# A two-layer stack of four mixers on one core: small first loads, a split first pass, and a new order in the even layer

## The chip, the cores and the metric

The kernel runs on one core of a Trainium2 chip. Its time is the device time of one execution in microseconds (us). The profile is one further execution, taken by the hardware profiler. Engines are PE (TensorE matmul), PEld (its weight loads), DVE (VectorE), ACT (ScalarE), POOL (GpSimd) and SP (which issues most transfers here).

## The reference, cut to what matters

256 tokens of width 2048, in float32, pass through two blocks. The first block has an even layer and an odd layer; the second has a differential attention, an S5 mixer, and an MLP behind each of the two. The change touches mostly the even layer:

```
z = _rmsnorm(x, norm_g) @ w_in                       # 2048 -> 7168
a_val, a_gt, a_gate, q, k, v, b_gate = split(z)      # 1024 columns each
u = a_val * sigmoid(a_gt)                            # with b_glu added to both
y = causal depthwise convolution of u over the tokens, 31 taps, + b_dw
y = silu(layernorm(y)) @ w_pw + b_pw                 # layernorm over 1024 channels
ya = y * silu(a_gate)
yb = causal softmax attention of 8 heads of 128 over 256 tokens * silu(b_gate)
x = x + concat(ya, yb) @ w_out
...
x = x + relu(rmsnorm(x) @ w1)**2 @ w2                # each MLP: 2048 -> 8192 -> 2048
```

## The kernel before, in words

**Products.** Every large product is made of three fp32r passes: a weight W and an activation A are each split into a rounded high part and a low remainder, and hi*hi + hi*lo + lo*hi is summed in PSUM. ACT makes the high part of the weights (`WH`, line 981), DVE the low part (`WL = RAW - WH`, line 1523). The activations are called `A1h`/`A1l` (first half of the kernel), `A3h`/`A3l` (second MLP), `Bh`/`Bl` (the squared ReLU inside an MLP) and so on.

**Weight stream.** The weights come in chunks of 4 x 128 rows by 512 columns (1 MB), into a ring of NR = 4 buffers `RAW`, in a fixed order written out by calls of `weights(tag, ...)`. Each chunk is used in two halves of 2 x 128 rows; a half is what PE works off at a time, and the split parts lie in a ring of RS = 4 halves. There are 948 halves. A tag names one product of 512 output columns: `gt0`, `val0`, `gt1`, `val1`, `q0`, `k0`, `v0`, `q1`, `k1`, `v1`, `bg0`, `bg1`, `ag0`, `ag1` (8 halves each), `pw0`, `pw1` (4 each), `eo0` to `eo3` (8 each) are the even layer; `cq` is the first of the odd layer; `m1u20` and `m1d00` are of the second MLP, its up product (8 halves) and its down product (4 halves).

**Two shapes.** Where a tag has `fm=True` (features on the partitions) the weight tile is stationary and the 256 tokens stream past it: 24 passes of 256 columns for a half. This is what the change's title calls a token stream. Where `fm` is false the activation is stationary and 512 weight columns stream: 12 passes of 512 columns for a half. In each MLP two `fm` products (`u`) alternate with four of the other shape (`d`).

**Order of the side work.** Everything that isn't a weight product is a generator of steps. `beside(steps)` appends them, and after each half `gemm` takes `STEPS[tag]` steps from it. PE, ACT and DVE each run the same program of halves and steps in their own queue and meet on semaphores. In DVE and ACT the split of half n+3 stands ahead of step n. The convolution is 31 steps for each half of the channels, one tap for four channel groups in a step (`convolution(nb)`, line 1683 in the profile, by `stt` at line 1531); it begins with `gt1`. The eight heads (`HEADS_E`) run in `bg1` and `ag0`, the layer norm over the channels (`LN_E`) in `ag1`. `rows(ph, T)` turns the 1/rms of the tokens, which lie on partitions, into a row: DVE makes `DG` (line 1527), PE multiplies it with ones, DVE copies the result into `RB` (line 1591). For the odd layer this is called inside `cq`, after its second half (`soon`).

**Start.** SP loads x in four pieces of 512 columns, with the first two chunks of weights between them. PE turns each 128 x 128 block of x (line 528) into a PSUM tile `T`; ACT writes `A1h` from it and DVE `A1l`.

Of the kernel before, what the change touches and what calls it, by code (L numbers as in the profile page):

```python
# [65 lines left out]
def build_program(nc, t):  # L66
# [229 lines left out]
    for i in range(2):  # L296
        weights(f"ag{i}", we, 2048, 2048 + 512 * i, fm=True, steps=(2, 1)[i])
# [54 lines left out]
    w_in = [sig(f"w_in{i}") for i in range(NR)]  # L352
    w_hi = sig("w_hi")
# [7 lines left out]
    x_in = [sig(f"x_in{i}") for i in range(4)]  # L361
    c_id, c_cols, c_row, c_row2 = sig("c_id"), sig("c_cols"), sig("c_row"), sig("c_row2")
# [100 lines left out]
    def pe(e):  # L463
        half, side, on_pair = itertools.count(), [iter(())], {}

# [14 lines left out]
        def gemm(tag, Ah, Al, ready=None, soon=None):  # L480
# [7 lines left out]
            for h in range(kts // 2):  # L488
                n = next(half)
                e.wait_ge(*w_lo[n])  # L490
                for j in range(2):
# [25 lines left out]
                if soon is not None and h == 1:  # L517
                    soon()
                step(STEPS[tag])

# [31 lines left out]
        for blk in range(2):  # L552
            e.wait_ge(*x_in[blk]["x"])
            for p in (2 * blk, 2 * blk + 1):
                norm_turn("e", p)

        def first():
            for what, k in (s or ("", 0) for s in FIRST):
                if what == "turn":
                    e.wait_ge(*x_in[k // 2]["x"])  # L560
                    norm_turn("e", k)
                elif what == "rows":
                    rows("e", TB[0])
                yield

# [16 lines left out]
        gemm("bg0", A1h, A1l)  # L582

        def heads_e():
            for what, h in HEADS_E:
                pT = SC[:, 2 + h % 2, :]
                if what == "scores":
                    T = TB[h % 2]
                    if h == 0:
                        e.wait_ge(*ev_d["k1", 1])  # L590
                        e.wait_ge(*ev_a["v1", 1])
                    if h >= 2:
                        e.wait_ge(*s_in["e", h - 2])
                    mm(T[:, 0:128], QTe[:, h, 0:128], KTe[:, h, 0:128], True, True)
                    mm(T[:, 128:384], QTe[:, h, 128:256], KTe[:, h, :], True, True).then_inc(*s_mm.up(("e", h)))
                elif what == "turn":
                    if h >= 1:
                        e.wait_ge(*p_c["e", h - 1])
                    turn_p(TB[2], SC[:, h % 2, :], ("e", h))
                else:  # L600
                    T = TB[3]
                    if h >= 1:
                        e.wait_ge(*o_d["e", h - 1])
                    e.wait_ge(*p_c["e", h])
# [3 lines left out]
                yield  # L608

        beside(heads_e())  # L610
        gemm("bg1", A1h, A1l)
        gemm("ag0", A1h, A1l)
        finish()

        def ln_e():
            for what, _ in LN_E:
                if what in ("mean", "var"):
# [5 lines left out]
                    for c in range(8):  # L623
                        m = mm(T[:, 0:256], ONES, src[:, c, :], c == 0, c == 7)
# [1912 lines left out]
```

## Time and profile before

| what | value |
|---|---|
| median of 3 runs | 2995.95 us (2992.68 to 2997.68) |
| the profiled execution's own time | 2997.26 us |
| its span in the trace | 2995.5 us |
| granted TensorE clock, mean | 0.992 of 2.4 GHz |
| PE busy | 2913.8 us, 97% |
| DVE busy | 1880.8 us, 63% |
| ACT busy | 1456.3 us, 49% |
| moved by DMA | 550.05 MB, mean 184 GB/s |

The span runs from the first instruction to the last. Times in the rows below count from its start. A busy PE is not a PE at its peak: a pass is recorded from its start to its end, and passes overlap, so that two passes that start 0.11 us apart each show 0.28 us.

### The profile page before, as it was taken

What the parts mean: (1) busy time and instruction counts of PE and PEld (TensorE: products, weight loads), DVE (VectorE), ACT (ScalarE), POOL (GpSimd) and SP (SyncE); (2) the same over time, 40 slices, a digit from 0 to 9 for tenths busy, and PEclk for the clock granted to TensorE, in tenths of its full rate; (3) what the DMA queues carried; (4) which work ended last, traced back from release to release, by engine and by line L of the source; (5) the groups of instructions that cost most, each with busy time, mean ns of one, the idle gap of its engine ahead of it and who ended that gap; (6) DMA issues with size and microseconds to landing.
All of it is one profiled execution on the core that took longest, in us unless ns stands there. A gap on an engine that the chain in (4) does not pass through costs nothing.

```text
span 2995.5 us, 45332 instructions
## 1 busy us (share of the span) xinstructions
PE 2913.8 (97%) x19056; PEld 2656.7 (89%) x19056; DVE 1880.8 (63%) x2604; ACT 1456.3 (49%) x1998; POOL 388.5 (13%) x444
## 2 busy tenths in 40 slices
PE   8999899999999999999999999998999999999998
PEld 8999888998899998989998899788889999999996
DVE  5997565775565655786565665666555555555555
ACT  5334554555455555444444446467544444444443
POOL 0000000000000000068457640033000000000000
PEclk9999999999999999999999999999999999999999
DMA  6555355551555555577666665533555555555553
GB/s 234 170 193 186 113 183 172 193 183 44 183 184 175 175 172 177 176 236 236 217 229 222 232 216 185 200 132 118 197 184 182 194 186 183 197 195 186 194 185 126
DMA packets 266570, 550.05 MB, mean 184 GB/s; under 512 B 9152, under 2 KB 13376, under 8 KB 266112
## 3 DMA queue, kind: packets, MB, share of 16 engines
q1 hardware_dynamic: 260192, 522.88, 52.7%
q0 software_dynamic: 5456, 21.73, 1.9%
q8 instruction: 151, 2.47, 0.3%
q10 hardware_dynamic: 720, 2.55, 0.3%
q14 instruction: 51, 0.42, 0.0%
HBM read 526.15 MB, written 20.97 MB: 183 GB/s over the span
## 4 chain that ended last, share of the span: by engine, by line
PE 83%; DVE 10%; ACT 3%; DMA 2%; issue 1%; SPq 0%; ACTq 0%; POOL 0%; DVEq 0%
PE G L478 77%; PE T L478 5%; DVE WL L1523 4%; DVE Y L1531 3%; DMA RD<-s_r 2%; ACT WH L981 1%; PE T L528 1%; ACT US L978 1%; DVE TC L1523 0%; DVE US L2154 0%; DMA X<-in_x 0%; ACT T L984 0%; DVE X L1531 0%; DVE SQ L1531 0%; DVE X L1523 0%
## 5 line engine op out<-in xcount | busy, mean ns | idle before, releaser
L1523 DVE TENSOR_TENSOR WL<-RAW,WH 128x1024 fp32r<-128x1024 f32 (+1 forms) x948 | 1178.0, 1251 | 807.6 <-ACT WH L981 796.7
L981 ACT ACTIVATE WH<-RAW 128x1024 fp32r<-128x1024 f32 (+1 forms) x948 | 992.7, 1055 | 1064.2 <-PE G L478 1060.1
L478 PE MATMUL G<-A1h,WH 128*128 128x256 f32 x2560 | 725.5, 283 | 9.2 <-DVE WL L1523 9.1
L478 PE MATMUL G<-A1h,WL 128*128 128x256 f32 x2560 | 717.9, 280 | 0.0
L478 PE MATMUL G<-A1l,WH 128*128 128x256 f32 x2560 | 717.9, 280 | 0.0
L478 PEld LDWEIGHTS G<-A1h,WH 128*128 128x128 f32 x2560 | 486.5, 190 | 12.2 <-DVE WL L1523 10.5
L478 PEld LDWEIGHTS G<-A1h,WL 128*128 128x128 f32 x2560 | 487.1, 190 | 0.0
L478 PEld LDWEIGHTS G<-A1l,WH 128*128 128x128 f32 x2560 | 485.0, 189 | 0.9
L478 PE MATMUL G<-WH,Bh 128*128 128x512 f32 x1024 | 399.7, 390 | 0.8 <-DVE WL L1523 0.8
L478 PE MATMUL G<-WH,Bl 128*128 128x512 f32 x1024 | 398.8, 390 | 0.0
L478 PE MATMUL G<-WL,Bh 128*128 128x512 f32 x1024 | 398.8, 389 | 0.0
L478 PE MATMUL G<-A3h,WH 128*128 128x256 f32 x1024 | 287.4, 281 | 0.0
L478 PE MATMUL G<-A3l,WH 128*128 128x256 f32 x1024 | 287.3, 281 | 0.0
L478 PE MATMUL G<-A3h,WL 128*128 128x256 f32 x1024 | 287.2, 280 | 0.0
L478 PEld LDWEIGHTS G<-WH,Bh 128*128 128x128 f32 x1024 | 192.3, 188 | 40.3 <-DVE WL L1523 1.2
L478 PEld LDWEIGHTS G<-WH,Bl 128*128 128x128 f32 x1024 | 192.3, 188 | 39.9
L478 PEld LDWEIGHTS G<-WL,Bh 128*128 128x128 f32 x1024 | 192.3, 188 | 39.0
L478 PE MATMUL G<-WH,A1h 128*128 128x512 f32 (+1 forms) x512 | 204.7, 400 | 5.6 <-DVE VAR L1523 3.3
L478 PE MATMUL G<-WH,A1l 128*128 128x512 f32 (+1 forms) x512 | 200.1, 391 | 0.0
L478 PE MATMUL G<-WL,A1h 128*128 128x512 f32 (+1 forms) x512 | 198.9, 388 | 0.0
L478 PEld LDWEIGHTS G<-A3h,WL 128*128 128x128 f32 x1024 | 196.1, 192 | 0.0
L478 PEld LDWEIGHTS G<-A3h,WH 128*128 128x128 f32 x1024 | 192.8, 188 | 0.2
(319 smaller groups left out, 3641.7 us busy)
## 6 DMA issues: line engine op xcount, KB each, us to landing
RAW<-in_mlp_w SPq DMA_DIRECT2D x256, 1024.0 KB, 5.4
RAW<-in_even_w_in SPq DMA_DIRECT2D x56, 1024.0 KB, 5.1
RAW<-in_a_w_in SPq DMA_DIRECT2D x48, 1024.0 KB, 5.1
RAW<-in_b_w_glu SPq DMA_DIRECT2D x32, 1024.0 KB, 5.3
RAW<-in_odd_w_in SPq DMA_DIRECT2D x20, 1024.0 KB, 5.0
RAW<-in_even_w_out SPq DMA_DIRECT2D x16, 1024.0 KB, 5.1
RAW<-in_odd_w_out SPq DMA_DIRECT2D x16, 1024.0 KB, 5.0
RAW<-in_a_w_out SPq DMA_DIRECT2D x16, 1024.0 KB, 5.0
```

Of the source, the lines that this page charges most:

```text
L478: return e.matmul(out, lhsT, rhs, start=start, stop=stop, skip_group_check=True)
L528: m = e.transpose(T[:, 256 * j + 128 * i:256 * j + 128 * i + 128], X[:, i, c:c + 128], IDENT)
L978: return e.activation(out, in_, func, scale=scale, bias=bias)
L981: return e.activation(out, in_, ACT.Copy, scale=scale, bias=0.0)
L1523: return e.tensor_tensor(out, a, b, op)
L1531: return e.scalar_tensor_tensor(out=out, in0=a, scalar=s, in1=b, op0=op0, op1=op1)
```

## The change

It has five parts.

1. **Split first pass.** When an `fm` product follows one that isn't, its very first pass of 256 columns is issued as two passes of 128 columns with the same weights. This happens at 21 places: `q1`, `bg0`, `gate0`, `aq0` to `aq3`, `m0u00`, `m1u00`, and `u20` to `u70` of both MLPs.
2. **Start.** x comes in eight pieces of 256 columns, and each of the first four chunks in two halves, so that a piece of x and half a chunk alternate. Only the identity and 16 columns of gains are loaded ahead; the other constants are issued by ACT after its fourth split. PE turns two pairs of blocks instead of four ahead of the first product. The statistics of x (squares, scale, rows) come after the last block is turned, and reach into `val0`.
3. **Even layer's steps.** All tags have one step a half. The convolution's 62 steps get two empty ones between them. From `bg0` on there are 32 steps: the layer norm's are steps 3 to 8, head h's scores are step 9 + 2h, its transposition step 11 + 2h, its product with V step 12 + 2h, and the split of the layer norm's result steps 27 and 28.
4. **rows** is in two parts; DVE makes `DG` directly behind `norm_scale`.
5. **soon** is called after the third half of `cq`, not the second.

The taps of the convolution are on VectorE in both kernels.

```diff
-        weights(f"gt{i}", we, 2048, 1024 + 512 * i, fm=True, steps=(2, 1)[i])
-        weights(f"val{i}", we, 2048, 512 * i, fm=True, steps=i)
+        weights(f"gt{i}", we, 2048, 1024 + 512 * i, fm=True, steps=1)
+        weights(f"val{i}", we, 2048, 512 * i, fm=True, steps=1)
...
-    FIRST = (("sq", 0), None, ("sq", 1), ("turn", 4), ("turn", 5), ("turn", 6), ("turn", 7), ("sq", 2), ("sq", 3),
-             ("scale", 0), ("rows", 0))
-    HEADS_E = [s for h in range(9) for s in ((("scores", h),) if h < 8 else ()) +
-               ((("turn", h - 1), ("pv", h - 1)) if h else ())]
-    LN_E = (("mean", 0), ("center", 0), ("center", 4), ("var", 0), ("out", 0), ("split", 0), ("out", 4), ("split", 4))
+    FIRST = [("turn", p) for p in range(2, 8)]
+    STATS = [("turn", p) for p in range(4, 8)] + [("sq", 0), ("sq", 1), ("sq", 2), ("sq", 3), ("scale", 0), None, None,
+                                                  ("rows", 0), ("gate", 0)]
+
+    HEADS_E = [[] for _ in range(32)]
+    for _n, _s in ((3, ("mean", 0)), (4, ("center", 0)), (5, ("center", 4)), (6, ("var", 0)), (7, ("out", 0)),
+                   (8, ("out", 4)), (27, ("split", 0)), (28, ("split", 4))):
+        HEADS_E[_n].append(_s)
+    for _h in range(8):
+        HEADS_E[11 + 2 * _h].append(("turn", _h))
+        HEADS_E[12 + 2 * _h].append(("pv", _h))
+        HEADS_E[9 + 2 * _h].append(("scores", _h))
...
-                            mm(o, hi[:, ws], Ah[:, kt, :], begin and s % 2 == 0, False)
+                            if begin and s == 0 and not last_fm[0]:
+                                mm(o[:, 0:128], hi[:, ws], Ah[:, kt, 0:128], True, False)
+                                mm(o[:, 128:256], hi[:, ws], Ah[:, kt, 128:256], False, False)
+                            else:
+                                mm(o, hi[:, ws], Ah[:, kt, :], begin and s % 2 == 0, False)
...
-                if soon is not None and h == 1:
+                if soon is not None and h == 2:
                     soon()
                 step(STEPS[tag])
+            last_fm[0] = fm
...
-        for blk in range(2):
-            e.wait_ge(*x_in[blk]["x"])
-            for p in (2 * blk, 2 * blk + 1):
+        for p in range(2):
+            e.wait_ge(*x_in[p]["x"])
+            norm_turn("e", p)
+
+        def first():
+            for _, p in FIRST:
+                e.wait_ge(*x_in[p]["x"])
                 norm_turn("e", p)
-
-        def first():
-            for what, k in (s or ("", 0) for s in FIRST):
-                if what == "turn":
-                    e.wait_ge(*x_in[k // 2]["x"])
-                    norm_turn("e", k)
-                elif what == "rows":
-                    rows("e", TB[0])
-                yield
+                yield
+            for _ in range(4):
+                yield
+            e.wait_ge(*c_one["c"])
+            rows("e", TB[0])
+            yield
 
...
+                    elif what == "scores":
+                        T = TB[h % 2]
+                        if h == 0:
+                            e.wait_ge(*d_step["ln_out", 4])
+                            e.wait_ge(*ev_d["k1", 1])
+                            e.wait_ge(*ev_a["v1", 1])
+                        if h >= 2:
...
-        e.dma_start(CID[:, :], t["consts"][:, 0:256]).then_inc(*c_id.up("c", 16))
-        e.dma_start(CV[:, 0:NCOLS], t["cols"]).then_inc(*c_cols.up("c", 16))
-        e.dma_start(PARITY, t["consts"][:, 1280:1282]).then_inc(*c_par.up("c", 16))
-        e.wait_ge(*c_cols["c"])
+        e.dma_start(IDENT, t["consts"][:, 0:128]).then_inc(*c_id.up("c", 16))
+        e.dma_start(CV[:, 0:16], t["cols"][:, 0:16]).then_inc(*c_gain.up("c", 16))
...
         def rows(ph, T):
+            rows_diagonal(ph)
+            rows_taken(ph, T)
+
+        def rows_diagonal(ph):
             for i in range(2):
                 d = ts(DG[:, 128 * i:128 * i + 128], IDENT, NS[:, 12 + i:13 + i], None, ALU.mult)
             d.then_inc(*d_step.up((ph, "dg")))
+
+        def rows_taken(ph, T):
             e.wait_ge(*r_mm[ph])
...
+                if j == (15, 0)[nb]:
+                    yield
...
-
-
-        gemm("cq", soon=lambda: rows("o", TB[0]))
+        rows_diagonal("o")
+
+
+        gemm("cq", soon=lambda: rows_taken("o", TB[0]))
...
-        for k in range(4):
-            e.dma_start(X[:, :, 512 * k:512 * k + 512], xv[:, :, 512 * k:512 * k + 512]).then_inc(*x_in[k].up("x", 16))
-            if k < 2:
-                load(k)
+        for p in range(8):
+            e.dma_start(X[:, :, 256 * p:256 * p + 256], xv[:, :, 256 * p:256 * p + 256]).then_inc(*x_in[p].up("x", 16))
+            c, h = p // 2, 2 * (p % 2)
+            e.dma_start(raw_view(c)[:, h:h + 2, :], chunks[c][0][:, h:h + 2, :]).then_inc(
+                *(w_in[c].up(c, 16) if h else w_first[c].up("c", 16)))
```

**Where the order moves.** PE at the start of `m1u20`, the first product of the second MLP's third round, behind the last passes of `m1d03` (`G2`, `G3` are banks of PSUM). Before:

```order
L478 MATMUL G3<-WH,Bh10 128x512
L478 MATMUL G3<-WL,Bh10 128x512
L478 MATMUL G3<-WH,Bl10 128x512
L478 MATMUL G0<-A3h,WH 128x256
L478 MATMUL G0<-A3l,WH 128x256
```

And in the changed kernel:

```order
L488 MATMUL G2<-WH,Bl10 128x512
L488 MATMUL G3<-WH,Bh10 128x512
L488 MATMUL G3<-WL,Bh10 128x512
L488 MATMUL G3<-WH,Bl10 128x512
L488 MATMUL G0<-A3h,WH 128x128 x2
L488 MATMUL G0<-A3l,WH 128x256
```

The pass that opens bank `G0` is now two passes of half the width; nothing else differs there.

DVE from the last tap of the convolution on (`Y<-U,CV,Y`), through `bg0`, to the first head (`SC_e<-T,MK_e` is the first instruction of its softmax). Before, ten splits of weights and the take of `bg0` stand ahead of the first head:

```order
L1531 SCALAR_TENSOR_TENSOR Y<-U,CV,Y 128x256 x4
L1523 TENSOR_TENSOR WL<-RAW,WH 128x1024 x10
L1523 TENSOR_TENSOR BG<-G,RB 128x512 x2
L1523 TENSOR_TENSOR WL<-RAW,WH 128x1024
L1531 SCALAR_TENSOR_TENSOR SC_e<-T,MK_e 128x384
L1598 TENSOR_REDUCE ST<-SC_e 128x1 x2
L1603 RECIPROCAL ST<-ST 128x2
L1527 TENSOR_SCALAR SC_e<-SC_e,ST 128x128
```

In the changed kernel (`SC_e<-T 128x256` takes the mean, the first `Y<-Y,SC_e` subtracts it; behind these rows come the variance, its root and the scaling):

```order
L1542 SCALAR_TENSOR_TENSOR Y<-U,CV,Y 128x256 x4
L1534 TENSOR_TENSOR WL<-RAW,WH 128x1024 x4
L1538 TENSOR_SCALAR SC_e<-T 128x256
L1534 TENSOR_TENSOR WL<-RAW,WH 128x1024
L1534 TENSOR_TENSOR Y<-Y,SC_e 128x1024
L1534 TENSOR_TENSOR WL<-RAW,WH 128x1024
L1534 TENSOR_TENSOR Y<-Y,SC_e 128x1024
L1534 TENSOR_TENSOR WL<-RAW,WH 128x1024
L1539 TENSOR_SCALAR SC_e<-T 128x256
L1584 RECIPROCAL SC_e<-SC_e 128x256
L1534 TENSOR_TENSOR SC_e<-SC_e 128x256 x2
```

The layer norm now stands ahead of the heads, and its instructions lie between the splits of `bg0` and `bg1`.

DVE between the last step of `norm_scale("o")` and the copy into `RB` (line numbers 1523, 1527, 1591 become 1534, 1538, 1608). Before:

```order
L1523 TENSOR_TENSOR NS<-NS 128x2 x2
L1523 TENSOR_TENSOR WL<-RAW,WH 128x1024 x2
L1527 TENSOR_SCALAR DG<-CID,NS 128x128 x2
L1591 COPY RB<-T 128x256
L1523 TENSOR_TENSOR WL<-RAW,WH 128x1024 x3
```

And in the changed kernel:

```order
L1534 TENSOR_TENSOR NS<-NS 128x2 x2
L1538 TENSOR_SCALAR DG<-CID,NS 128x128 x2
L1534 TENSOR_TENSOR WL<-RAW,WH 128x1024 x3
L1608 COPY RB<-T 128x256
L1534 TENSOR_TENSOR WL<-RAW,WH 128x1024 x2
```

`DG` has moved ahead of the splits, and the copy, which waits for PE, stands behind three splits instead of two.

## Rows read from the trace of the kernel before

**Rows 1.** The page: busy time, the chain, and the split on ACT.

```profile
PE 2913.8 (97%) x19056; PEld 2656.7 (89%) x19056; DVE 1880.8 (63%) x2604; ACT 1456.3 (49%) x1998; POOL 388.5 (13%) x444
...
PE 83%; DVE 10%; ACT 3%; DMA 2%; issue 1%; SPq 0%; ACTq 0%; POOL 0%; DVEq 0%
...
L981 ACT ACTIVATE WH<-RAW 128x1024 fp32r<-128x1024 f32 (+1 forms) x948 | 992.7, 1055 | 1064.2 <-PE G L478 1060.1
```

**Rows 2.** Windows, PE alone: `m1u10`, then `m1u20`, then `m1u21`.

```profile
2319.07:2340.83 21.76, 21.76 (x194) 1.00 0.60 195
2406.03:2428.75 22.72, 22.72 (x193) 1.00 0.60 192
2428.75:2451.36 22.61, 22.61 (x194) 1.00 0.56 188
```

**Rows 3.** Timeline of PE where `m1u20` begins.

```profile
2406.03 0.39 PE L478 MATMUL G<-WH,Bl 128*128 128x512 f32 x1
2406.26 0.28 PE L478 MATMUL G<-A3h,WH 128*128 128x256 f32 x1
```

**Rows 4.** Timeline of PE, 128-column transposes behind `oo3`.

```profile
827.17 1.09 PE L528 MATMUL T<-CID,X 128*128 128x128 f32 x8 [0.95 <-DVE X L1523]
```

**Rows 5.** Timeline of the start, all engines.

```profile
7.05 1.28 ACT L981 ACT_TABLE_LOAD   x1 [7.05 <-PE T L528]
...
11.07 2.36 DVE L1523 TENSOR_TENSOR WL<-RAW,WH 128x1024 fp32r<-128x1024 f32 x2
...
11.36 1.97 PE L528 MATMUL T<-CID,X 128*128 128x128 f32 x8 [3.54 <-DMA X<-in_x]
...
12.98 0.56 PE L478 MATMUL G<-A1h,WH 128*128 128x256 f32 x1
```

**Rows 6.** Windows: PE at the start, and at one drop of the clock.

```profile
13.60:17.00 3.40, 3.40 (x18) 1.00 1.05 386
37.50:40.90 3.40, 3.40 (x18) 0.50 0.17 26
```

**Rows 7.** Waits of PE from 0 to 44.2 us.

```profile
PE T L478 <- DVE DG L1527: 3.3, 1, 3.3
```

**Rows 8.** Waits of PE, `q0` to `v1`, 109.4 to 246.7 us.

```profile
PE G L478 <- DVE WL L1523: 4.2, 5, 1.9
```

**Rows 9.** Timeline of DVE during the convolution.

```profile
110.03 1.22 DVE L1523 TENSOR_TENSOR WL<-RAW,WH 128x1024 fp32r<-128x1024 f32 x1
111.16 1.67 DVE L1531 SCALAR_TENSOR_TENSOR Y<-U,CV,Y 128x256 f32<-128x256 f32 x4
```

**Rows 10.** Windows, PE alone, `bg0` to `pw0`.

```profile
246.72:383.40 136.68, 123.93 (x985) 0.99 0.42 139
```

**Rows 11.** Waits of PE in the same stretch.

```profile
PE T L478 <- ACT SC_e L981: 8.5, 4, 3.4
PE G L478 <- DVE PWl L1523: 2.7, 2, 2.1
```

**Rows 12.** Timeline of PE, the layer norm's sum over channels.

```profile
340.58 3.62 PE L478 MATMUL T<-Y,CID 128*128 128x256 f32 x16
```

**Rows 13.** Timeline of DVE, root and scaling of the layer norm.

```profile
356.39 0.42 DVE L1528 TENSOR_SCALAR SC_e<-T 128x256 f32<-128x256 f32 x1 [1.61 <-PE T L478]
357.37 1.75 DVE L1573 RECIPROCAL SC_e<-SC_e 128x256 f32<-128x256 f32 x1 [0.55 <-ACT SC_e L978]
```

**Rows 14.** Timeline of DVE, first and last instructions of one softmax.

```profile
308.78 0.56 DVE L1531 SCALAR_TENSOR_TENSOR SC_e<-T,MK_e 128x384 f32<-128x384 f32 x1 [1.99 <-PE T L478]
...
311.24 0.55 DVE L1527 TENSOR_SCALAR SC_e<-SC_e,ST 128x128 f32<-128x128 f32 x2
```

**Rows 15.** Timeline of DVE in `cq`.

```profile
490.99 2.36 DVE L1523 TENSOR_TENSOR WL<-RAW,WH 128x1024 fp32r<-128x1024 f32 x2
493.26 0.48 DVE L1527 TENSOR_SCALAR DG<-CID,NS 128x128 f32<-128x128 f32 x2
```

**Rows 16.** Windows, PE alone, `cq`'s third half.

```profile
494.90:498.30 3.40, 3.40 (x10) 0.50 0.53 145
```

More of the change, by code:

```diff
@@ L296, in build_program @@
     for i in range(2):
-        weights(f"ag{i}", we, 2048, 2048 + 512 * i, fm=True, steps=(2, 1)[i])
+        weights(f"ag{i}", we, 2048, 2048 + 512 * i, fm=True, steps=1)
     for i in range(2):
@@ L352, in build_program @@
     w_in = [sig(f"w_in{i}") for i in range(NR)]
+    w_first = [sig(f"w_first{i}") for i in range(NR)]
     w_hi = sig("w_hi")
@@ L581, in pe @@
             gemm(f"v{i}", A1h, A1l, None)
-        gemm("bg0", A1h, A1l)
         def heads_e():
[L585 to L604, printed above, removed]
-                    mm(T[:, 0:256], Ve[:, 0, 128 * h:128 * h + 128], pT[:, 0:256], True, False)
-                    mm(T[:, 128:256], Ve[:, 1, 128 * h:128 * h + 128], pT[:, 256:384], False, True).then_inc(
-                        *pv_mm.up(("e", h)))
@@ L608, in heads_e @@
                 yield
         beside(heads_e())
[L611 to L617, printed above, removed]
-                    T, src = (TB[0], Y) if what == "mean" else (TB[1], BG)
-                    if what == "mean":
-                        e.wait_ge(*conv[7, 30])
-                    else:
-                        e.wait_ge(*a_step["ln", 4])
-                    for c in range(8):
-                        m = mm(T[:, 0:256], ONES, src[:, c, :], c == 0, c == 7)
-                    m.then_inc(*t_mm.up(("ln", what)))
-                yield
@@ L628, in pe @@
-        beside(ln_e())
-        gemm("ag1", A1h, A1l)
+        for i in range(2):
+            gemm(f"bg{i}", A1h, A1l)
+        for i in range(2):
+            gemm(f"ag{i}", A1h, A1l)
         finish()
@@ L990, in split_next @@
             N = chunks[c][1][1]
[L991 to L992 removed]
+            if h == 0 or c < NR:
+                e.wait_ge(*(w_first[c]["c"] if c < NR and h == 0 else w_in[c % NR][c]))
             if n >= RS:
@@ L1001, in gemm @@
                     split_next()
-                if soon is not None and h == 1:
+                if soon is not None and h == 2:
                     soon()
@@ L1103, in act, with first @@
                 a.then_inc(*act2.up((f"gt{nb}", i)))
+        def first():
+            for what, k in (s or ("", 0) for s in STATS):
+                if what == "sq":
+                    squares("e", k, x_in[2 * k]["x"], x_in[2 * k + 1]["x"])
+                elif what == "turn":
+                    norm_high("e", k, A1h, even_gain)
+                elif what == "scale":
+                    root(NS[:, 10:12], NS[:, 8:10], "e")
+                elif what == "gate":
+                    e.wait_ge(*c_cols["c"])
+                    yield
+                    gate(0)
+                yield
+        beside(first())
+        for nb in range(2):
+            gemm(f"gt{nb}")
+            if nb:
+                gate(nb)
             gemm(f"val{nb}")
@@ L1154, in act @@
-        beside(ln_e())
-        gemm("ag1")
-        silu_fm("ag1", GA, 4)
+        for i in range(2):
+            gemm(f"bg{i}")
+            silu_fm(f"bg{i}", BG, 4 * i)
+        for i in range(2):
+            gemm(f"ag{i}")
+            silu_fm(f"ag{i}", GA, 4 * i)
         finish()
@@ L1551, in gemm @@
                     split_next()
-                if soon is not None and h == 1:
+                if soon is not None and h == 2:
                     soon()
@@ L1648, in first @@
                 elif what == "scale":
+                    e.wait_ge(*c_id["c"])
                     norm_scale("e", 3)
+                    rows_diagonal("e")
                 elif what == "rows":
-                    rows("e", TB[0])
+                    rows_taken("e", TB[0])
+                elif what == "gate":
+                    gate(0)
                 yield
@@ L1671, in dve @@
             gemm(f"gt{nb}")
-            for i in range(2):
-                e.wait_ge(*whole_bank(f"gt{nb}", i))
-                tt(SG[:, 2 * i:2 * i + 2, :], pairs(G_of[f"gt{nb}"][i][:, :]), RB2, ALU.mult).then_inc(
-                    *ev_d.up((f"gt{nb}", i)))
+            if nb:
+                gate(nb)
             gemm(f"val{nb}")
+            if nb == 0:
+                e.wait_ge(*c_cols["c"])
             for i in range(2):
@@ L1743, in dve @@
-        beside(ln_e())
-        gemm("ag1")
-        take_fm("ag1", GA, 4)
+        for i in range(2):
+            gemm(f"bg{i}")
+            take_fm(f"bg{i}", BG, 4 * i)
+        for i in range(2):
+            gemm(f"ag{i}")
+            take_fm(f"ag{i}", GA, 4 * i)
         finish()
```

215 lines of the change are left out of this document (110 added, 105 removed).

## Prediction

> **What bounds the kernel.** I read the page first: PE is busy for 97% of the span, and 83% of the chain that ended last is PE's [rows 1]. So time can be won only where PE waits, where its clock is low, or where its passes stand further apart than they must. Windows over single products measure the last. A product of eight halves whose tokens stream has 192 passes; `m1u10` takes 21.76 us, 113.3 ns a pass, while `m1u20` and `m1u21`, the same instructions on other weights, take 22.72 and 22.61 us, 118 ns a pass, at full clock and with no wait [rows 2]. At the seam `m1u20` begins 0.23 us behind the last wide pass, so nothing was idle there [rows 3]. I went through the starts of passes of the whole trace: the pace is one of these two, and it is kept from product to product until something interrupts. In both MLPs all twelve pairs `u20`/`u21` to `u70`/`u71`, which follow directly on a wide product, run slow; `m1u00` to `m1u11`, which follow on transposes, run fast. Then I read PE's waits by stretch: 3.3 us for `DG` at the start [rows 7], 4.2 us for weight splits by DVE under the convolution [rows 8], 8.5 and 2.7 us around heads and layer norm [rows 11].
>
> **The clock.** Before 17 us PE shows 18 passes in 3.4 us, just as in the stretch with a granted clock of 0.50 behind the wait for `DG` [rows 6]; that is 1.2 GHz, though the row at the start prints 1.00. At 2.4 GHz 30 would fit. A drop of 3.4 us so costs 1.7 us of work. One follows the 3.3 us wait, one stands in `cq` [rows 16].
>
> **1. Split first pass: 21.1 us, if it works.** Twelve pairs would win 22.72 + 22.61 - 2 x 21.76 = 1.81 us each, 21.7 us [rows 2]. `bg0` (8 halves) and the first five of `gate0` run slow as well: 13 x 24 passes x 4.7 ns = 1.4 us. The price is one more pass at 21 places. No 128-column fp32r pass is in the trace. The nearest row is the eight 128-column transposes, 1.09 us in all, some 0.11 us from start to start [rows 4]; two short passes then take 0.22 instead of 0.12 us, 2.1 us for 21 places. Bounds: below, the pair costs what one pass does, nothing; above, 0.23 us each, a wide pass's own pace [rows 3], 7 us for all. Nearest is the transpose, so 2.1. What isn't certain is whether the pace changes. For it: the three products that begin behind 128-column transposes, `aq0`, `m0u00` and `m1u00`, all end in the fast pace, and `q1` and `aq1` to `aq3`, which follow a wide product whose passes were a few ns uneven, fell back to it within five passes. Against it: behind the short interruptions inside `bg1`, `ag0`, `gate0` and `aq1` both paces come up, about evenly. The twelve seams are alike to the nanosecond, so they go together.
>
> The Trainium skill, "TensorE: Matmul & The Clock Gate", section "Back-to-back issue gap", gives the distance of passes as a function of their width alone: N/2.4 + 2.5 ns, 109 ns for 256 columns. By that rule the two paces would not exist and the edit could only cost: rival B's outcome. The trace doesn't agree: same width, 113.3 and 118 ns.
>
> **2. Start: 6.5 us.** In the trace the first product waits for x's second piece: PE idles 3.54 us for it and begins at 12.98 [rows 5]. Ahead of this it now needs two pieces of 256 KB and half a chunk, 1 MB where it was 2 MB. Then the chain of compute decides: the table load behind the first transposes (1.28 us), two copies (0.4 each, estimated from the split, which is four times as wide), the split on ACT 1.05 and on DVE 1.2 [rows 1, 5]. With x there at 4.1 us (its first piece, twice as large, was turned a little over 1 us ahead of the table load at 7.05) this gives 4.1 + 1.1 + 1.3 + 0.8 + 1.05 + 1.2 = 9.6; I take 9.7, so 3.3 us earlier. Bounds: 1 us if the small pieces bring nothing but the order, 4 us at most. The statistics leave `gt0`: the wait for `DG`, 3.3 us [rows 7], and its drop of the clock, 1.7 us, go. `DG` is now asked for after the third half of `val0`; counting ACT's work from the last transposes on (four splits, four squares of 1.25) it comes about 0.5 us late. Two more pairs of transposes stand behind the first pass: 0.9. The chain transposes, `A1h`, split, split is 3.1 us against PE's 3.17 for a half with its transposes, so it just holds; 0.4 for friction. 3.3 + 3.3 + 1.7 - 0.5 - 0.9 - 0.4 = 6.5. If the granted clock rises no earlier than it did, 1.7 less.
>
> **3. Two empty convolution steps: 3.2 us.** A split takes 1.13 us from start to start and four taps 1.59 [rows 9]: 2.72, just PE's half. DVE can't catch up what the takes of `val`, `q` and `k` cost it, and PE waits five times, 4.2 us [rows 8]. Two steps without taps give 2 x 1.59 = 3.2, all of it inside those waits.
>
> **4. Layer norm ahead of the heads: 3 us.** `bg0` to `pw0` takes 136.7 us with 985 passes [rows 10]. Its 36 halves need 97.9, the 32 passes of both channel sums 7.0 (16 in 3.62 us) [rows 12], each head seven short and four longer passes, 7 x 0.11 + 4 x 0.22 = 1.65, so 13.2: 118.1 in all. 18.6 us are lost now. What will be lost: the first scores wait for the scaled `Y`. From the end of the variance sum DVE needs 4.5 us to the inverse root (0.4, the root on ACT, 1.75 for the reciprocal, four small ones) [rows 13], 1.15 for a split, 1.2 for half of `Y`, which is as wide; ACT then has four SiLUs (2.0), `bg0`'s SiLU (1.15) and a split (1.0), all of 1024 columns, estimated from the split's 1.05 with something for each further instruction; DVE a split and the other half, 2.4. That is 13.4 us, and PE has three halves, 8.2: it waits 5.3 us, and the clock falls, 1.7. Then the heads. A softmax holds DVE for 3.0 us [rows 14]; with two splits, the product with the gate and ACT's copy between, a head takes 7.5 us, PE 2 x 2.72 + 1.65 = 7.1. Half a microsecond a head is lost once the lead of some 3 us is used up: 2 us; 1.1 at the first transposition, 2.1 behind `bg1`'s take and 3.3 behind `ag0`'s, where SiLU and table loads stand ahead of the copies that PE waits for. Sum 15.5, so 3.1 less than now, and `pw0` has its operands early. I take 3. Bounds: all waits hidden, 18; every term half as large again, a loss of 5.
>
> **5. `DG` and `soon` in `cq`: 3.7 us.** `DG` stands behind two splits, 2.27 us [rows 15], and PE asked for it a half earlier. Now it is ready before; I count 2.0 for the wait and 1.7 for the drop of the clock [rows 16]. Bounds 2 and 4.
>
> **Sum.** 21.1 + 6.5 + 3.2 + 3 + 3.7 = 37.5. The profiled execution's own time was 2997.26; it lies 1.3 above the median. 2997.3 - 37.5 - 1.3 = 2958.5.
>
> **Rivals.**
> A. All as above: 2958.5, own range 2948 to 2967 (terms 2 and 4 at their bounds, not both). Chance 0.62.
> B. The pace does not change. Then 21.7 + 1.4 are missing, the extra passes stay: 37.5 - 23.1 = 14.4, so 2981.6. For it: after the short passes come the same 256-column passes, and interruptions inside `gate0` left it slow. Against it: the three fast starts behind transposes. Chance 0.23.
> C. The pace changes at some seams only, or turns slow where it was fast (`m1u00` to `m1u11`, `q1`, `aq0`): 2965 to 2976. Chance 0.08.
> D. Slower than before: the clock. From the first scores on PE stops once a head, and if it is granted 1.2 GHz through these 22 halves and their own passes, some 75 us of work at full clock, up to 75 us are added; it decides from 26 drops of 3.4 us on (37.5 + 6 at 1.7 each). With all of it: 3030. For it: a 3.3 us wait did bring one drop [rows 6, 7]. Against it: this stage has four waits for `SC_e`, up to 3.4 us, and a mean clock of 0.99 [rows 10, 11]. Chance 0.03.
> What is left, 0.04, is a time under 2948.
>
> **Range and chances.** 2948 to 2985 holds A, B and C but for their ends. A measurement of this kernel can tell 0.2%, 6 us, from no change. Faster by more: A, C, nearly all of B and the rest, 0.91. Within it: the low end of B with a bad stage 4, 0.05. Slower: 0.04.
>
> **What the profile after would show.** `m1u20` and `m1u21` in 21.8 us each behind a first pair of short passes (else B). The first product at 9 to 10.5 us, and no 0.50 clock near 37 us. The wait for splits under the convolution near 1 us. One wait of 4 to 6 us ahead of the first scores, released by DVE's `Y`, with a drop of the clock behind it; heads 7.1 to 7.6 us apart. In `cq` no wait for `DG` and no drop. The forecast is wrong above all if the pace stays, and then by 23 us.

## Result and the profile after

The changed kernel takes 2965.88 us (median of 4 runs, 2960.78 to 2968.59), the kernel before 2996.81 (2992.68 to 2997.72) on the same chip: ratio 0.9898, 95% interval 0.9885 to 0.991. It is 31 us faster; 37.5 had been forecast. The profiled execution took 2968.59 us, its span is 2966.8, 28.7 less than before. The page of its profile, where it answers to [rows 1]:

```profile
PE 2900.3 (98%) x19077; PEld 2643.4 (89%) x19077; DVE 1884.3 (64%) x2604; ACT 1455.2 (49%) x1997; POOL 388.7 (13%) x444
...
PE 86%; DVE 8%; ACT 3%; DMA 2%; issue 1%; ACTq 0%; POOL 0%; DVEq 0%
```

PE holds more of the chain and has 21 passes more (19056 to 19077), yet is busy for 13.5 us less: the passes stand closer. To see where the time went I cut both traces at the ends of the same products. Windows of PE in the changed kernel, in this order: start to `val1`; `q0` to `v1`; `bg0` to `pw1`; `cq`; `ckv` to `av3`; `ao0` to `m0u11`; `m0d00` to `gl0`; `m1u00` to `m1u11`; `m1d00` to the end (the `eo` and the other `gl`, `gg` products, left out, didn't move by more than 0.05). Columns as in [rows 2]: stretch; its length, PE busy, passes; granted clock; DMA share; GB/s.

```profile
0.00:106.82 106.82, 98.65 (x804) 1.00 0.67 223
106.82:239.12 132.30, 131.88 (x963) 1.00 0.58 186
239.12:384.79 145.67, 137.33 (x1083) 0.96 0.45 153
474.56:499.04 24.48, 23.53 (x110) 1.00 0.45 137
499.04:1106.49 607.45, 606.38 (x4152) 1.00 0.49 164
1106.49:1300.91 194.42, 186.78 (x1212) 1.00 0.58 191
1300.91:2092.72 791.81, 767.77 (x5036) 0.98 0.60 203
...
2249.26:2343.32 94.06, 91.28 (x778) 0.96 0.54 180
2343.32:2966.75 623.43, 610.37 (x3849) 0.99 0.55 185
```

The same windows of the kernel before:

```profile
0.00:109.42 109.42, 96.72 (x804) 0.98 0.63 215
109.42:246.72 137.30, 133.09 (x962) 1.00 0.55 182
246.72:394.28 147.56, 134.81 (x1081) 0.99 0.44 147
484.09:512.20 28.11, 25.39 (x109) 0.94 0.37 118
512.20:1118.72 606.52, 605.45 (x4148) 1.00 0.49 164
1118.72:1314.84 196.12, 187.46 (x1212) 0.99 0.58 192
1314.84:2113.39 798.55, 774.77 (x5031) 0.99 0.60 201
...
2269.92:2362.61 92.69, 89.91 (x778) 0.98 0.56 182
2362.61:2995.45 632.84, 619.81 (x3843) 0.99 0.55 183
```

The differences, line by line: -2.60, -5.00, -1.89, -3.63, +0.93, -1.70, -6.74, +1.37, -9.41; together 28.7. So half of the gain, 14.8 us, lies in the last three rows, which hold the MLPs' twelve pairs, and the start, forecast with 6.5, brought 2.6. The pair of [rows 2] in the changed kernel is in the first two windows of PE (`m1u20`, then `m1u21`); behind them the two pieces of one drop of the clock behind the first scores, and a second drop in `ag1`:

```profile
2386.74:2408.74 22.00, 22.00 (x195) 1.00 0.60 195
2408.74:2430.50 21.76, 21.76 (x195) 1.00 0.56 192
278.90:282.30 3.40, 2.74 (x11) 0.50 0.81 252
282.30:285.70 3.40, 3.40 (x18) 0.50 0.15 57
347.15:350.55 3.40, 3.40 (x18) 0.50 0.53 199
```

22.72 and 22.61 us have become 22.00 and 21.76. The first of the two windows, here and in [rows 2], starts with the last wide pass of `m1d03`, 0.23 us, and stops short of the last pass of `m1u20`; the window of `m1u10`, 21.76, holds no wide pass. From first pass to first pass, `m1u20` took 21.88 us in the changed kernel (first row) and 22.61 before (second row):

```profile
2386.97:2408.85 21.88, 21.88 (x195) 1.00 0.60 195
2406.26:2428.87 22.61, 22.61 (x194) 1.00 0.60 192
```

So the product with the split first pass takes 0.12 us more than the 21.76 of a fast one without it. The seam, in PE's timeline, beside [rows 3]:

```profile
2386.74 0.39 PE L488 MATMUL G<-WH,Bl 128*128 128x512 f32 x1
2386.97 0.33 PE L488 MATMUL G<-A3h,WH 128*128 128x128 f32 x2
2387.14 0.33 PE L488 MATMUL G<-A3l,WH 128*128 128x256 f32 x1
2387.31 0.28 PE L488 MATMUL G<-A3h,WL 128*128 128x256 f32 x1
```

From the first short pass to the second full one are 0.34 us, where two fast passes take 0.23; from there on the passes are 0.11 us apart. This accounts for it. The start, PE, beside [rows 5]:

```profile
10.10 0.58 PE L488 MATMUL G<-A1h,WH 128*128 128x256 f32 x1 [1.02 <-DVE WL L1534]
```

The chain is the one forecast: transposes, the table load (5.71 to 6.99), copies and a split on ACT, the split on DVE, whose end the first pass waited for. It began 0.4 us later: x's first piece was turned from 4.54 on. Waits of PE, first from 0 to 62 us (beside [rows 7]), then from 239.1 to 384.8 (beside [rows 11]):

```profile
PE T L543 <- DMA X<-in_x: 6.9, 2, 4.5
```

```profile
PE T L488 <- DVE Y L1534: 5.2, 1, 5.2
PE T L488 <- ACT SC_e L992: 2.9, 1, 2.9
```

There is no wait for `DG` left at the start, and one new wait of 5.2 us ahead of the first scores. In `q0` to `v1` PE waits 0.4 us for a split, where it was 4.2 [rows 8].

### The profile page after: what moved, and what is told of

It reads as the page before. It is cut to its first block, busy times and chain, and to the rows that moved or that the text cites. A ratio compares the mean times of both kernels' runs of the same rounds, so it can differ in the third digit from the quotient of the medians.

```text
span 2966.8 us, 45387 instructions
## 1 busy us (share of the span) xinstructions
PE 2900.3 (98%) x19077; PEld 2643.4 (89%) x19077; DVE 1884.3 (64%) x2604; ACT 1455.2 (49%) x1997; POOL 388.7 (13%) x444
## 4 chain that ended last, share of the span: by engine, by line
PE 86%; DVE 8%; ACT 3%; DMA 2%; issue 1%; ACTq 0%; POOL 0%; DVEq 0%
PE G L488 80%; PE T L488 4%; DVE WL L1534 3%; DMA RD<-s_r 2%; DVE Y L1542 2%; ACT WH L992 1%; PE T L543 1%; ACT US L989 1%; DVE US L2175 0%; DVE TC L1534 0%; ACT SC_e L995 0%; DVE X L1542 0%; DVE X L1534 0%; ACT T L995 0%; DVE ST L1615 0%
## 5 line engine op out<-in xcount | busy, mean ns | idle before, releaser
L488 PE MATMUL G<-A3h,WH 128*128 128x256 f32 (+1 forms) x1031 | 284.2, 277 | 0.0
L488 PEld LDWEIGHTS G<-A3l,WH 128*128 128x128 f32 x1024 | 193.2, 189 | 0.0
```

Of the source, the lines that this page charges most:

```text
L488: return e.matmul(out, lhsT, rhs, start=start, stop=stop, skip_group_check=True)
```

## Experiments

Twelve kernels were run. Those with one run serve for their traces, product by product, since executions of one kernel differ by up to 10 us; medians are compared for the others.

**The split alone, and all but the split.** The first adds part 1 to the kernel before; the second takes it from the changed one, so that its fast pairs must go.

```diff
-                            if begin and s == 0 and not last_fm[0]:
-                                mm(o[:, 0:128], hi[:, ws], Ah[:, kt, 0:128], True, False)
-                                mm(o[:, 128:256], hi[:, ws], Ah[:, kt, 128:256], False, False)
-                            else:
-                                mm(o, hi[:, ws], Ah[:, kt, :], begin and s % 2 == 0, False)
+                            mm(o, hi[:, ws], Ah[:, kt, :], begin and s % 2 == 0, False)
```

> The kernel before with the split first pass alone. Theory S (the short pass sets the pace): the twelve u pairs behind wide products take 21.99 + 21.76 us as in the changed kernel, 1.58 less than before each, 19 us in all; bg0 wins about 0.8, aq1 to aq3 lose about 0.8 together; 18.5 to 20 us less than before, 2976 to 2979. Theory N (the pace changed because the work ahead of the products was moved): the pairs stay at 22.72 + 22.61 and the time is that of before or 2 us more.

> The changed kernel without the split. Theory S: all twelve pairs fall back to 118 ns a pass and the time rises by 18 to 20 us over the changed kernel, to 2983 to 2986, so that all other parts together are worth 10 to 13 us. Theory N: the pairs stay at 113 ns and the time stays within 2 us of the changed kernel.

Measured: the split alone 2978.13 us (2976.93 to 2982.24), ratio 0.9936 (0.9923 to 0.995); without it 2983.03 (2981.97 to 2986.04), ratio 0.9949 (0.9936 to 0.9961). Windows of PE, split alone: `bg0` to `pw1`, `m1u20`, `m1u21`.

```profile
246.50:393.40 146.90, 134.10 (x1082) 0.99 0.44 148
2395.14:2417.13 21.99, 21.99 (x194) 1.00 0.62 194
2417.13:2438.89 21.76, 21.76 (x194) 1.00 0.57 194
```

Without the split: `bg0` to `pw1`, the drop of the clock behind the first scores and the stretch after it, `m1u00` to `m1u11`, `m1u20`, `m1u21`.

```profile
238.89:380.86 141.97, 133.00 (x1081) 0.99 0.46 155
...
278.75:282.15 3.40, 2.94 (x12) 0.50 0.84 290
282.20:285.60 3.40, 3.40 (x32) 1.00 0.03 11
...
2251.25:2347.26 96.01, 93.23 (x778) 0.98 0.54 177
...
2390.69:2413.41 22.72, 22.72 (x193) 1.00 0.59 190
2413.41:2436.02 22.61, 22.61 (x194) 1.00 0.56 189
```

The pace goes with the split, in both directions. A pair gains 22.72 + 22.61 - 21.99 - 21.76 = 1.58 us, twelve of them 19.0. Rival B is out. `m1u00` to `m1u11`, which begin behind transposes, run slow here as well (96.01 us against 94.06). In all ten traces with the first pass split there they are fast; of the four without it only the kernel before has them fast. So the split seems to help there too, but there the pace isn't fixed by it alone. Parts 2 to 5 alone took 15.3 us off the span (2995.5 to 2980.2), where 10 to 13 had been expected before the run; the prediction's terms for them make 16.4.

**What about the split does it.** Five kernels put other passes at the seam. The first leaves the narrow product whole and halves the last 512-column pass of each MLP round ahead of it:

```diff
+                            if end and i == 1 and tag[0] == "m" and tag[2] == "d" and tag[4] == "3":
+                                mm(o[:, 0:256], Al[:, kt, tk], hi[:, 0:256], False, True)
+                                m = mm(o[:, 256:512], Al[:, kt, tk], hi[:, 256:512], False, True)
```

> The changed kernel without the split first pass; instead the last wide pass of each MLP's fourth down product is issued as two passes of 256 columns. One more pass at the same seam, but none shorter than its weight load. Theory S1 (the short pass makes PE wait for weights, and that sets the phase): the twelve pairs stay slow, 118 ns, about the time of the kernel without the split. Theory S2 (any additional pass shifts the phase): the pairs run at 113 ns and the time is within 2 us of the changed kernel.

The second splits at every product whose tokens stream:

```diff
-                            if begin and s == 0 and not last_fm[0]:
+                            if begin and s == 0:
```

> The changed kernel with the first pass split at every product whose tokens stream, also behind another such product. Theory S1: a product that begins slow behind a slow one turns fast: gt1, val1, ak1 to ak3, pw0, pw1, gate0's successors; about 0.85 us each where eight halves ran slow, 6 to 8 us in all, against 0.12 for each short pair (some 38 more); net 2 to 4 us faster than the changed kernel. If the outcome depends on the phase at which the short pass comes, some products that run fast now turn slow, and the net is between 4 us slower and 2 faster.

The third halves the pass behind the first as well, the fourth also the one behind that:

```diff
+                                mm(o[:, 0:128], hi[:, ws], Al[:, kt, 0:128], False, False)
+                                mm(o[:, 128:256], hi[:, ws], Al[:, kt, 128:256], False, False)
```

> The changed kernel with two extra passes at each place: the first pass and the one behind it (same weights, low part of the tokens) both as two of 128 columns. It tells what turns the pace of the 256-column passes from 118 to 113 ns. Theory P, the count: an extra pass, short or not, shifts the stream against something that alternates from pass to pass, so that one shifts it and two put it back; then the 12 pairs u20/u21 to u70/u71 of the two MLPs take 22.7 + 22.6 us again and the kernel is near 2984 us. Theory I, the interruption: any pass out of rhythm at the seam starts the fast pace; then they stay at about 22.2 + 21.8 us, and the kernel is 2 to 5 us above the changed one by the further passes.

> The changed kernel with the first three passes at each place (same 128 weight rows: high by high, high by low, low by high) all as two of 128 columns: three extra passes. Theory P (something alternates from pass to pass, an odd number of extra passes turns it and an even number doesn't): the 12 pairs of the MLPs are fast again, 21.76 us for u21 and 22.2 to 22.5 for u20, and the kernel is at 2968 to 2976. Rival (only one extra pass fits, or only the first pass being short): they stay at 22.6 us or more, and the kernel is at 2985 to 2995.

And the fifth leaves the first two whole and halves the third:

```diff
+                                mm(o[:, 0:128], lo[:, ws], Ah[:, kt, 0:128], False, False)
+                                m = mm(o[:, 128:256], lo[:, ws], Ah[:, kt, 128:256], False, False)
```

> The changed kernel with the third pass of each place (low weights by high tokens) split in two of 128 columns in place of the first: again one extra pass. The change's extra pass at the head of the product and e3_wide_halved's at the tail of the one before both brought the fast pace, two and three extra passes did not. If exactly one extra pass at the seam is what counts, wherever it stands, the 12 pairs are fast: u21 21.76 us, kernel 2958 to 2969. If it matters that the pass out of rhythm stands where the wide product ends and the narrow one begins, they are slow: u21 22.6 us, kernel 2984 to 2992.

Measured, windows of PE: wide pass halved (2969.03 us), `m1d03` and `m1u20`,

```profile
2376.85:2387.84 10.99, 10.99 (x51) 1.00 0.61 193
2387.84:2409.62 21.78, 21.78 (x194) 1.00 0.61 194
```

two extra passes (2992.70 us), `m1u21`,

```profile
2423.08:2445.69 22.61, 22.61 (x194) 1.00 0.53 187
```

three extra passes (2990.38 us), `m1u21`,

```profile
2419.96:2442.58 22.62, 22.62 (x195) 1.00 0.55 187
```

and the third pass split (2967.56 us), `m1u21`.

```profile
2407.56:2429.32 21.76, 21.76 (x195) 1.00 0.55 194
```

At these twelve seams one extra pass starts the fast pace, whether it stands last in the wide product or first or third in the narrow one, and whether the pieces have 256 or 128 columns. Pieces of 256 columns are as long as the other passes, so a pass shorter than usual isn't what does it. Two extra passes leave it slow: "any interruption will do" falls. Three leave it slow as well: so does my theory of odd and even, which had forecast 2968 to 2976. What remains is a rule of thumb with no mechanism.

The weight loads show one more thing. Each pass has its own load, and three kinds of pass take turns: high weights with high tokens, high with low, low with high. Loads inside the pair `m1u20`, `m1u21` (count, then busy time in us and mean ns of one): before, the low weights; in the changed kernel, the same; with three extra passes, the high weights with high tokens.

```profile
L478 PEld LDWEIGHTS G<-A3h,WL 128*128 128x128 f32 x119 | 22.9, 192 | 0.0
L488 PEld LDWEIGHTS G<-A3h,WL 128*128 128x128 f32 x124 | 23.3, 188 | 0.0
L488 PEld LDWEIGHTS G<-A3h,WH 128*128 128x128 f32 x122 | 23.4, 192 | 0.0
```

In a fast pair every load has a mean of 188 ns. In a slow one, one kind in three has 192: the low weights with no and two extra passes, the high weights with three. So the pattern of a pair at 118 ns repeats every three passes, and there is more than one such pattern. Whether the longer load is the cause or a sign of it, no run tells. A period of three passes is also a rival that I did not test: no and three extra passes agree at all three kinds of seam (these twelve, `aq1` to `aq3`, `gate0`), but one extra pass does not act alike in first and third place behind `av0` and `ckv`. Four extra passes were not run.

Behind other products the rule reads otherwise, by the starts of passes: `aq1`, which follows `av0`, begins fast with no extra pass, slow with its first pass split, fast with two or three extra or with its third pass split; `gate0`, behind `ckv`, begins slow with none or the first split, fast with two, slow with three, and fast with the third pass split.

The times missed some expectations, mostly for reasons outside the pairs. With the wide pass halved the kernel was 3 us above the changed one, not within 2: `m1u00` to `m1u11` ran slow. Two extra passes gave 2992.70 where 2984 had been expected; by the granted clock that trace has 55.6 us at 0.50, the one without the split 37.7. The split everywhere (2965.83 us, one run) made `ak1` to `ak3` fast, 0.7 us each, but brought nothing in all, where 2 to 4 us had been expected: each further split costs 0.12 us (`m1u21` took 21.88 us). `ak0` was fast in it too, but also in the kernel without the split.

**Convolution.** Without the two empty steps.

```diff
-                if j == (15, 0)[nb]:
-                    yield
```

> The changed kernel without the two convolution steps that hold no taps. My theory (term 3: DVE can't catch up with its own pace of 2.72 us a step, so each split that it owes is waited for): PE's waits for weight splits under q, k and v come back, some 3 us, and the seven products q0 to v1 take about 3 us longer than in the changed kernel (132.3 us). Rival: the waits were fed by the old start, whose statistics and row scales stood in gt0, and the new start alone gave DVE the lead; then q0 to v1 take the same to within 0.5 us, and the two empty steps are worth nothing. Outside this stretch no more than 2 us either way.

Measured: 2967.30 us, one run. Window of PE, `q0` to `v1`:

```profile
105.38:240.89 135.51, 134.18 (x963) 1.00 0.55 182
```

The stretch takes 3.2 us longer, as term 3 had it, but that proves little. PE waits for splits only 1.3 us there, and 1.7 us are `q1` and `k1` at the slow pace. `e6_diagonal_late`, which keeps the empty steps, took as long, 135.30 us, below: with no wait and the slow pace up to `v1`. `v1` ends at 240.89 here and between 237.8 and 241.2 in the kernels with the new start that have the empty steps. What they are worth is within this spread; left open.

**`DG` in `cq`.** One kernel makes the diagonal behind the splits again but keeps the hook at the third half; the other keeps the diagonal early and puts the hook back at the second, in the queues of PE, ACT and DVE alike.

```diff
-        rows_diagonal("o")
-        gemm("cq", soon=lambda: rows_taken("o", TB[0]))
+        gemm("cq", soon=lambda: rows("o", TB[0]))
```

```diff
-                if soon is not None and h == 2:
+                if soon is not None and h == 1:
```

> The changed kernel with the odd layer's diagonal DG back inside the hook of cq, behind the weight splits, the hook itself still at the third half. My theory (the place of DG in DVE's order is what PE waited for): cq again has a wait for DG of about 2 us and a drop of the clock behind it, and takes 3.6 us longer than the 24.48 us of the changed kernel. Rival: the half that the hook moved back is enough (DVE's two splits, 2.3 us, end inside PE's 2.7 us), and cq stays at 24.5 us, so that the diagonal's early place does nothing.

> The changed kernel with cq's hook back at the second half, the diagonal still made ahead of cq's splits. It is the other half of the pair with e6_diagonal_late (24.93 us for cq). If the early diagonal alone is enough too, cq stays within 0.5 us of 24.48; if DVE's column copy behind it then holds up a split, up to 1 us more; if only the later hook took the wait away, cq is at 27 to 28 us as before. My expectation is the first.

Measured: 2966.29 and 2959.94 us, one run each. Windows of PE with the diagonal late: `q0` to `v1`, `cq`; then its wait for `DG`.

```profile
105.89:241.19 135.30, 135.30 (x964) 1.00 0.56 187
475.14:500.06 24.92, 23.79 (x109) 1.00 0.43 134
```

```profile
PE T L488 <- DVE DG L1538: 0.2, 1, 0.2
```

With the hook early: `cq`.

```profile
471.31:495.79 24.48, 23.53 (x110) 1.00 0.46 139
```

Either edit alone removes the wait; my expectation of 3.6 us for the first was wrong, since PE, asking one half later, leaves DVE the 2.3 us for its splits: what is left of the wait is 0.2 us. Term 5's size was right, and it had two causes of which one was enough.

**The wait ahead of the heads.** Heads and the last splits two half-steps later, layer norm where it is; then the same with the first pass split at all streaming products but `aq1` to `aq3`.

```diff
-                   (8, ("out", 4)), (27, ("split", 0)), (28, ("split", 4))):
+                   (8, ("out", 4)), (29, ("split", 0)), (30, ("split", 4))):
...
-        HEADS_E[11 + 2 * _h].append(("turn", _h))
-        HEADS_E[12 + 2 * _h].append(("pv", _h))
-        HEADS_E[9 + 2 * _h].append(("scores", _h))
+        HEADS_E[13 + 2 * _h].append(("turn", _h))
+        HEADS_E[14 + 2 * _h].append(("pv", _h))
+        HEADS_E[11 + 2 * _h].append(("scores", _h))
```

> The changed kernel with all eight heads (scores, turn, product with V) and the two splits of the pointwise operand two half-steps later, the layer norm where it is. My theory: the 5.2 us wait ahead of the first scores is three halves of PE against 13 us of DVE and ACT; two more halves, 5.4 us, cover it, the drop of the clock at 279 us (6.8 us long, 3.4 us lost) goes with it, and pw0 loses some 1 to 3 us because its splits now end one or two halves ahead of it. In all 5 to 8 us less than the changed kernel, ratio to before about 0.987. Rival 1: the wait moves: DVE and ACT are as late at the second and third head, PE waits there, and the time stays within 2 us of the changed kernel. Rival 2: the clock drops come with the stalls that each head brings anyway (one head needs 7.5 us of DVE and ACT against 7.1 of PE), so the wait goes and a drop stays: 5 us of wait less, 3.4 us not.

> The heads two half-steps later (as e7_heads_two_later), and the first pass split at every product whose tokens stream, but for aq1, aq2 and aq3, whose split turned them slow. If the two add up: e7's 2958.7 less 0.71 us for each of ak1 to ak3 (read from e4_split_everywhere) and 0.2 to 0.3 us for the first halves of aq1 to aq3, 3 us in all: 2955 to 2957, ratio to before about 0.986. If the pace that comes behind the transposes in these products is decided anew each time, the further splits bring nothing: 2958 to 2960.

Measured: 2958.67 us (2957.73 to 2961.80), ratio 0.9871 (0.9854 to 0.9887); and 2959.33 (2957.05 to 2960.55), ratio 0.9874 (0.9858 to 0.9891). Windows of PE, heads later: start to `val1`, `q0` to `v1`, `bg0` to `pw1`.

```profile
0.00:103.99 103.99, 95.74 (x803) 1.00 0.68 226
103.99:238.14 134.15, 131.79 (x963) 1.00 0.57 186
238.14:377.52 139.38, 133.16 (x1083) 1.00 0.47 158
```

The wait for `Y` is gone, the granted clock of the stretch is 1.00 where it was 0.96, and the stretch is 6.3 us shorter. In its place PE waits 3.1 us for weight splits there; DVE's work is the same, and I take it that PE only met it elsewhere. The median is 7 us lower, which is the 5 to 8 us expected, against both rivals, though the intervals of the ratios overlap by a little (0.9885 to 0.9887). How much of it is the drops of the clock depends on the execution: in the nine other traces with the heads at their first new place the stretch took 141.97 to 146.02 us, in both with the heads later 139.38 and 140.68.

The further splits bring nothing that can be measured on top, though not for the reason given: they held, and brought in the trace 3.1 us in `ckv` to `av3` (604.59 against 607.66), but a drop of the clock came back in `bg1` (140.68 against 139.38), and `m0d00` to `gl0` took 790.03 against 787.68.

## Why the prediction was right, and where it was off

**Direction and pace.** Case A came, 7.4 us above its forecast and just inside its own range. The time alone could not tell it from C, whose range begins at 2965; that the pairs are fast, as A has it, is read from the trace. The step that carried it, that an extra pass behind a wide product ends the slow pace, held at all twelve seams alike, and B and D did not come. It rested on three products behind transposes, two of which turn slow again behind later interruptions (`aq0` in its seventh half, `m0u00` in its fifth). The reason was thinner than it looked, for two or three extra passes would have failed at the same seams: that one was the right number is luck. And it had a small other side, rival C in little: `aq1` to `aq3` lost their fast start, which with the extra passes is the 0.93 us that the row of `ckv` to `av3` lost.

**Term 1, 21.1 us.** The pairs measured 19.0. The step that was mis-sized is the gain of a pair, put at 1.81 us. It took the window of `m1u20`, which holds a wide pass, against that of `m1u10`, which holds none. From first pass to first pass, a slow pair takes 45.23 us and a fast one without an extra pass would take 43.5, so there were 1.70 us to win, and twelve pairs had 1.3 us less than forecast. The price of the extra pass was nearly right: 0.12 us, forecast with 0.1 from the transposes, 0.3 us in twelve pairs. `bg0` gained 0.7 with the split alone (22.73 to 22.00), and the row with `gate0` and the `aq` lost 0.9, so the whole term is 18.8; outside the pairs 0.5 us had been forecast and 0.2 were lost.

**Term 2, 6.5 us.** Measured 2.6 up to `val1`. The first product begins at 10.10 instead of 9.7, since x's first piece was there at 4.5, not 4.1. The wait for `DG` and its drop are gone, as said. What the sum had left out is the pace: in the profiled execution `val0` turns slow at its fourth half and stays so through `val1`, where before these products were fast. The same instructions came out either way: in six other kernels with the same start (both with later heads, split everywhere, wide pass halved, two and three extra passes) they are fast, and `val1` ends at 104.0 to 104.5: 4.9 to 5.4 us gained. But most of that is not kept: the kernel with later heads reaches `q0` 2.8 us earlier than the changed one and then waits for splits (134.15 us against 132.30), so that `v1` ends only 1 us earlier. DVE, busy with convolution and splits for 132.2 of these 132.3 us and for all but 0.1 of the 134.15 with later heads, sets the time there. Terms 2 and 3 can so be judged only together: 9.7 forecast, 7.6 measured, 8.6 with later heads.

**Term 3, 3.2 us.** The wait fell from 4.2 to 0.4 as forecast, and the row gained 5.0, but the experiment did not tell what the empty steps have to do with it. That the size came out is no proof of the reason.

**Term 4, 3 us.** Measured 1.2, against the split alone, which has the old order from `bg0` to `pw1` (146.90 to 145.67). The wait, forecast with 5.3, is 5.2 us; the sum from DVE's and ACT's rows was good. The clock was not: 1.7 us had been put down for one drop, and there are two, one twice as long, by the windows at 278.90, 282.30 and 347.15. At 0.50 that loses 5.1 us, 3.4 more than forecast. Against this, the waits for the copies that ACT makes, put at 6.5 us, measured 2.9: two errors of the same size had opposite signs. The 1.8 us that the term is short are not divided further. Without the split pass the wait was 5.2 us too, but one drop came, half as long, and the stretch took 141.97.

**Term 5, 3.7 us.** `cq` fell from 28.11 to 24.48, 3.6, with no drop left. In the kernel with the split alone the wait stood (1.8 us) and the drop had not come; `cq` took 26.53, which divides the term into 2.0 and 1.6, as forecast.

**What no term had.** Of the rows without an edit, `ao0` to `m0u11` gained 1.7 us, as a drop at 1300 us did not come; `m0d00` to `gl0` should have gained half of the pairs, 9.5, and gained 6.7; `m1u00` to `m1u11` lost 1.4, at clock 0.96 against 0.98. Together that is 2.4 us net. By the lengths of the drops 1.7 of them are the clock: one drop of 3.4 us fewer than before in the first of these rows, and 3.4 us more of half clock in each of the other two. The rest wasn't traced; the same instructions from `m0d00` to `gl0` took 791.81 here and 787.74 in the kernel with the early hook. The profiled execution was the slowest of its four; the median lies 2.7 us lower.

Summed over the profiled executions: 2.3 short in term 1, 2.1 in terms 2 and 3, 1.8 in term 4, 0.1 in term 5, and 2.4 in the rows that no term had, 8.7 in all, of 37.5 - 28.7 = 8.8. Two steps were wrong in kind: windows with different contents were compared in term 1, and clock drops were entered one per wait, each as short as the shortest seen.

## To carry to other kernels

Compare the start-to-start distance of equal passes in different products before anything else: here 4% of the time of 24 products was lost with no wait, no low clock and no idle engine, and one extra pass in the right place won it back. Compare from first pass to first pass, so that both stretches hold the same work. Find the place by trying, and check neighbouring products for the opposite effect. Where an engine sums up many small jobs (DVE with convolution, splits and layer norm), time won by its consumer is handed back as a wait further on, so sum such terms up to the end of that engine's load, not one by one. And a wait in front of a stage is removed more surely by starting the stage later than by hurrying its operands: here, two half-steps later took 6.3 us off the stretch.

## What the runs showed of the hardware

- The same 256-column fp32r passes run 113 or 118 ns apart at full clock and with no wait, and keep this distance over hundreds of passes. Behind the MLP's wide products no, two and three extra passes gave 118, one gave 113, each at all twelve seams; behind `av0` and `ckv` the pattern is another one. The Trainium skill, "TensorE: Matmul & The Clock Gate", section "Back-to-back issue gap", gives N/2.4 + 2.5 ns for an isolated pass, 109 ns for 256 columns, says that in a stream the weight loads count too, and names no second distance. The trace has two, both above 109. What the two states are stays open.
- In the pairs at 118 ns one of every three weight loads has a mean of 192 ns instead of 188; in those at 113 ns none has.
- Splitting a 256-column pass into two of 128 cost 0.12 us as the first pass of a product, about one full pass, with no column more to stream. Splitting the last 512-column pass in two of 256 cost some 0.03: the next product began 0.24 us behind the first piece instead of 0.23, and took 21.78 instead of 21.76 from first pass to first pass.
- The same wait of 5.2 us was followed by a drop of 6.8 us to 1.2 GHz in the changed kernel and of 3.4 us in the one without the split.
